# Seven products of quarters in place of eight for the q, k and v of each attention head

## What is computed

```
h = _rmsnorm(x, norm1_g[l])                      # 512 x 2048
proj = h @ w_in[l]
q, k, v, og, gkf, gkb, glu, ga, gb = jnp.split(proj, offsets, axis=-1)
qh = _to_heads(q, GLA_HEADS) * (GLA_DK ** -0.5)  # 4 heads of 256 columns
kh = _to_heads(k, GLA_HEADS)                     # 4 heads of 256
vh = _to_heads(v, GLA_HEADS)                     # 4 heads of 512
log_af = jax.nn.log_sigmoid(gkf @ gla_gk_fwd_w[l] + gla_gk_fwd_b[l]) / GLA_GATE_NORMALIZER
...
o_f = _gla_scan(qh, kh, vh, _to_heads(log_af, GLA_HEADS), False)
```

## Time and profile before

| | us |
|---|---|
| median of 3 runs | 4249.54 |
| lowest, highest | 4245.31, 4250.67 |
| the profiled execution's own time | 4248.95 |
| its span, first to last instruction | 4247.2 |
| TensorE busy in the span | 3640.4 (86%) |
| VectorE busy | 2771.0 (65%) |
| ScalarE busy | 921.1 (22%) |
| GpSimd busy | 1251.8 (29%) |
| TensorE in one of the four heads, q to the last output, head 0 | 29.73 to 164.26 |

### The profile page before, as it was taken

How to read it: one execution, slowest core, us unless ns; L and a number is a source line. 1 busy time by engine, 2 the same in 40 slices (tenths; PEclk the granted TensorE clock), 3 DMA queues, 4 the chain that set the end, 5 groups by cost and what they waited for, 6 DMA issues and landing times.

```text
span 4247.2 us, 39184 instructions
## 1 busy us (share of the span) xinstructions
PE 3640.4 (86%) x13406; PEld 2204.9 (52%) x13406; DVE 2771.0 (65%) x4163; ACT 921.1 (22%) x2049; POOL 1251.8 (29%) x768
## 2 busy tenths in 40 slices
PE   9999999999999989868699999789998777555555
PEld 3444479545766667645588886444443334211111
DVE  3233359102999999974866667875656878766666
ACT  2232210101222211132211121111111233233222
POOL 0000000000233332231223323233323555666665
PEclk9999999999999999889899999899999899899999
DMA  3111248888999999999999999999999999999998
GB/s 136 60 56 64 70 169 299 300 315 292 390 416 397 389 419 409 412 373 411 407 409 412 415 426 418 423 421 427 427 404 385 418 414 402 402 419 418 418 418 361
DMA packets 162496, 1488.41 MB, mean 350 GB/s; under 512 B 24512, under 2 KB 24640, under 8 KB 33344
## 3 DMA queue, kind: packets, MB, share of 16 engines
q0 software_dynamic: 81408, 948.08, 53.8%
q1 hardware_dynamic: 70704, 512.44, 31.0%
q10 hardware_dynamic: 10256, 26.35, 1.6%
HBM read 1465.82 MB, written 20.97 MB: 350 GB/s over the span
## 4 chain that ended last, share of the span: by engine, by line
PE 58%; DMA 27%; DVE 9%; issue 5%; ACT 1%; POOL 0%; SPq 0%; ACTq 0%; DVEq 0%; POOLq 0%
PE bank L1750 34%; DMA arena_c<-in_peer_uv_rest,arena_c 14%; PE bank L2081 6%; PE bank L1801 5%; PE bank L1854 5%; DVE arena_o L1436 4%; DMA wring<-in_peer_u_tiles 4%; DMA wring<-in_w_in 3%; DMA arena_c<-in_peer_uv,arena_c 3%; PE bank L1898 2%; PE bank L1816 1%; PE bank L1940 1%; DVE arena_c L1423 1%; DMA wring<-in_conv_w_pw 1%; DMA wring<-in_w_out 1%
## 5 line engine op out<-in xcount | busy, mean ns | idle before, releaser
L1750 PE MATMUL bank<-arena_h,wring 128*128 128x128 f32 (+5 forms) x6784 | 1408.4, 371 | 48.7 <-DMA wring<-in_w_in 19.1
L687 POOL DMA_INDIRECT arena_c<-in_peer_uv,arena_c x272 | 662.1, 2434 | 2599.4 <-DVE arena_o L1436 1526.1
L1750 PEld LDWEIGHTS bank<-arena_h,wring 128*128 128x128 f32 x6784 | 1049.1, 195 | 405.3 <-issue 135.5
L1423 DVE SCALAR_TENSOR_TENSOR arena_c<-arena_c 128x2048 f32<-128x2048 f32 (+1 forms) x512 | 915.1, 1787 | 291.0 <-DMA arena_c<-in_peer_uv_rest,arena_c 252.4
L1436 DVE SCALAR_TENSOR_TENSOR arena_o<-arena_c,arena_o 128x2048 f32<-128x2048 f32 (+1 forms) x511 | 944.5, 1848 | 222.0 <-ACT arena_c L862 163.9
L2111 PE MATMUL bank<-arena_c,cols 128*128 128x512 f32 x960 | 518.3, 668 | 358.2 <-ACT cols L1046 358.1
L2111 PEld LDWEIGHTS bank<-arena_c,cols 128*128 128x128 f32 x960 | 178.5, 204 | 673.9 <-ACT cols L1046 540.2
L2081 PE MATMUL bank<-wring,arena_h 128*128 128x512 f32 x1024 | 445.5, 594 | 17.0 <-DMA wring<-in_peer_u_tiles 17.0
L698 POOL DMA_INDIRECT cols<-dots,cols x240 | 339.2, 1414 | 116.0 <-issue 100.1
L856 ACT ACTIVATE arena_c<-arena_c 128x1 f32<-128x1 f32 x272 | 55.1, 203 | 1380.2 <-DVE arena_c L1423 1365.2
L2081 PEld LDWEIGHTS bank<-wring,arena_h 128*128 128x128 f32 x1024 | 192.6, 190 | 268.3 <-issue 234.3
(11 more groups left out here) (227 smaller groups left out, 2367.9 us busy)
## 6 DMA issues: line engine op xcount, KB each, us to landing
wring<-in_w_in SPq DMA_DIRECT2D x176, 1024.0 KB, 10.8
wring<-in_peer_u_tiles SPq DMA_DIRECT2D x64, 1024.0 KB, 17.6
wring<-in_w_out SPq DMA_DIRECT2D x48, 1024.0 KB, 9.9
wring<-in_peer_w_q SPq DMA_DIRECT2D x48, 1024.0 KB, 11.1
wring<-in_gla_w_o SPq DMA_DIRECT2D x32, 1024.0 KB, 11.3
wring<-in_conv_w_pw SPq DMA_DIRECT2D x32, 1024.0 KB, 12.7
wring<-in_w_v SPq DMA_DIRECT2D x16, 1024.0 KB, 4.9
wring<-in_w_ga SPq DMA_DIRECT2D x16, 1024.0 KB, 4.9
```

The costliest lines, as they stand in the source:

```text
L687: pool.indirect_dma_start(out=slot_of(n), out_offset=None, in_=uv_tab, in_offset=column(idx_cur, U % 2, k)).then_inc(landed(n)[0], 16)
L1423: V.scalar_tensor_tensor(row, row, 1.0, block_of(h2, n // P)[:, first:], ALU.mult, ALU.mult, accum_out=act_u[:, n % TOP:n % TOP + 1]).then ...
L1750: last = M(ps[bank][:, at:at + hi - lo], w_tile(slot)[:, k, :], act_in[:, k, lo:hi], start=k == 0, stop=k == KT - 1)
```

## The change

A product of two matrices, each cut in two by two quarters, takes eight products of quarters. The change computes it with seven, by Strassen's scheme in Winograd's form, for q, k and v of every head: the names P1 to P7 are the seven products, S1, S2, S4 sums of quarters of weights, h_1 to h_4 sums of quarters of `hT`, and U2, C11, C12, U3, C22, C21 the sums that make results.

- VectorE makes h_1 to h_4 once, behind the normalisation (2048 columns each).
- GpSimd makes four sums of 1024 columns for q, four for k, and four for each of two chunks of v, in every head. The fourth is written over a quarter of the tile itself.
- TensorE's seven products of q and of k are 8 matmuls of 256 columns each, those of v 16. They come in the order P1, P2, P5, P6, P3, P7, P4 and take the banks 4 to 7 in turn.
- ScalarE copies P1 and P5 out, and VectorE adds the others (`add_out`), 7 operations for each of q, k and v: of 256 columns for q and k, of 512 for v.
- The first load of the ring is four tiles in place of three, and the loads of v come in another order.

The core of the diff:

```diff
+            def weight_sums(n, set_of, a11, a12, a21, a22):
+                s1, s2, s4 = set_of
+                G.tensor_tensor(s1, a21, a22, ALU.add).then_inc(w_sum, 1)
+                pool.wait_ge(w_sum, n + 1)
+                G.tensor_tensor(s2, s1, a11, ALU.subtract).then_inc(w_sum, 1)
+                pool.wait_ge(w_sum, n + 2)
+                G.tensor_tensor(s4, a12, s2, ALU.subtract).then_inc(w_sum, 1)
+                G.tensor_tensor(a21, a11, a21, ALU.subtract).then_inc(w_sum, 1)
...
+                for chunk in range(2):
+                    slot = 2 * chunk
+                    pool.wait_ge(w_in_slot[slot], 16 * (turn + 1))
+                    pool.wait_ge(w_in_slot[slot + 1], 16 * (turn + 1))
+                    pool.wait_ge(mm, product_count(h, chunk, P3))
+                    weight_sums(h * SUMS + 8 + 4 * chunk, [by_cols(a) for a in sum_sets[chunk]],
...
-                for n in range(4):
-                    act.wait_ge(q_mm, h * 4 + (n + 1))
-                    dst = qT[:, n, :] if n < 2 else kT[:, n - 2, :]
-                    A(dst, ps[4 + n][:], ACT.Copy, scale=DK ** -0.5 if n < 2 else 1.0).then_inc(q_ev, 1)
+                for which in range(2):
+                    copy_out(which, P1, 0, 0)
+                    copy_out(which, P5, 1, 1)
...
                     act.wait_ge(z_qk, h * 4 + (u + 1))
-
-                for b in range(NB):
-                    act.wait_ge(v_mm, h * 4 + (b + 1))
-                    A(v_tok[:, b, :], ps[4 + b][:], ACT.Copy).then_inc(v_ev, 1)
+                    if u == 2:
+                        copy_out(2, P1, 0, 0)
+                copy_out(2, P5, 1, 1)
...
+            dve.wait_ge(n1_done, KT)
+            V.tensor_tensor(h_1, lower[:, :, token_half(1)], lower[:, :, token_half(0)], ALU.subtract).then_inc(n1_done, 1)
...
+                def add_out(which):
+                    dve.wait_ge(copied, h * COPIES + (2 * which + E1))
+                    add_product(which, U2, P6, (0, 0), (1, 0))
+                    add_product(which, C11, P2, (0, 0), (0, 0))
+                    dve.wait_ge(copied, h * COPIES + (2 * which + E5))
+                    add_quarter(which, C12_PART, (1, 0), (0, 1), (1, 1))
+                    add_product(which, C12, P3, (0, 1), (0, 1))
+                    add_product(which, U3, P7, (1, 0), (1, 0))
+                    add_quarter(which, C22, (1, 0), (1, 1), (1, 1))
+                    add_product(which, C21, P4, (1, 0), (1, 0))
...
+                def v_wait(n):
+                    if n < 4:
+                        added_by(1, (U2, C12, U3, C21)[n])
+                    if n == P3:
+                        copied_by(2, E1)
+                    if n == P7:
+                        added_by(2, C11)
+                    if n == P4:
+                        copied_by(2, E5)
...
+                first = seven(0, q_wait, (weight_half(0, 0), weight_half(0, 1), weight_half(1, 0), weight_half(1, 1)),
+                              sum_sets[0], lambda *to: half_product(*to, normed=h == 0))
+                if h:
+                    first[P1].then_inc(w_used, 1)
+                first[P4].then_inc(w_used, 1)
+                first = seven(1, k_wait, (weight_half(2, 0), weight_half(2, 1), weight_half(3, 0), weight_half(3, 1)),
+                              sum_sets[1], half_product)
+                first[P4].then_inc(w_used, 2)
```

More of the change, by code:

```diff
@@ L59 @@
 HEAD_TILES = 8
+HALF_TILE = TILE // 2
+(P1, P2, P5, P6, P3, P7, P4) = range(7)
+(E1, E5) = (1, 2)
+(U2, C11, C12_PART, C12, U3, C22, C21) = range(1, 8)
+PRODUCTS, COPIES, ADDS = 21, 6, 21
+SUMS = 16
 SB_GLU0 = HEADS * HEAD_TILES
@@ L270, in hybrid_block @@
         glow = take(T)
-        assert o_[0] <= SG, o_[0]
+        h_1, h_2, h_3, h_4 = (take(KT // 2, T // 2) for _ in range(4))
+        q_s4, k_s1 = take(HALF_TILE), take(HALF_TILE)
+        assert o_[0] <= SG + 1932, o_[0]
+        q_s1, q_s2 = (view(arena_o, (KT - 4) * T + n * HALF_TILE, HALF_TILE) for n in range(2))
+        pair_flat = pair_w.rearrange("p j t -> p (j t)")
+        k_s2, k_s4 = (pair_flat[:, n * HALF_TILE:(n + 1) * HALF_TILE] for n in range(2))
+        sum_sets = ((q_s1, q_s2, q_s4), (k_s1, k_s2, k_s4))
+        sq_flat = sq_o.rearrange("p e t -> p (e t)")
+        rstd_x = sq_flat[:, 0:T]
+        wgk = sq_flat[:, T:T + KT * (32 + RANK)].rearrange("p (k r) -> p k r", r=32 + RANK)
         sig0 = view(arena_c, RU, 2, 2, GL)
@@ L1732, in gate_ranks @@
                 for k in range(4 * c, 4 * c + 4):
-                    last = M(ps[6][0:32 + RANK, :], wgk[:, k, :], hT[:, k, :], start=k == 0, stop=k == KT - 1)
+                    last = M(ps[1][0:32 + RANK, :], wgk[:, k, :], hT[:, k, :], start=k == 0, stop=k == KT - 1)
                 last.then_inc(glow_mm, 1)
@@ L1773, in heads_sum @@
                 pe.wait_ge(o_added, h + 1)
[L1774 to L1785 removed]
+                M(ps[6][:], ones_d, sq_o[:, 0, :], start=True, stop=True).then_inc(o_stat, 1)
@@ new lines, in _, with seven @@
+            halves = hT[:, 0:KT // 2, :], hT[:, KT // 2:KT, :]
+            def seven(which, waits, weights, sums, product):
+                first = []
+                for n, (w, tokens) in enumerate((
+                        (weights[0], halves[0][:, :, token_half(0)]), (weights[1], halves[1][:, :, token_half(0)]),
+                        (sums[0], h_1), (sums[1], h_2), (sums[2], halves[1][:, :, token_half(1)]),
+                        (weights[2], h_3), (weights[3], h_4))):
+                    waits(n)
+                    first.append(product(w, tokens, bank_of(which, n), n))
+                return first
@@ L1793, in _ @@
                       start=True, stop=True).then_inc(z_mm, 1)
-                pe.wait_ge(q_ev, h * 4 + 4)
-                for s in range(4):
-                    tile_ready(4 + s, h, HEAD_TILES)
-                    for k in range(QUART):
-                        kk = s * QUART + k
-                        for b in range(NB):
-                            last = M(ps[4 + b][:], hT[:, kk, b * P:b * P + P], w_quart(s)[:, k, :],
-                                     start=kk == 0, stop=kk == KT - 1)
-                            if k == 0 and b == 0:
-                                last.then_inc(w_used, 1)
-                            if kk == KT - 1:
-                                last.then_inc(v_mm, 1)
+                first = seven(2, v_wait, [[weight_cols(n, j), weight_cols(n + 2, j)] for n, j in
+                                          ((0, 0), (1, 0), (0, 1), (1, 1))],
+                              [[sum_sets[n][i].rearrange("p (k c) -> p k c", c=DV // 2) for n in range(2)]
+                               for i in range(3)], v_product)
+                first[P1].then_inc(w_used, 1)
+                first[P4].then_inc(w_used, 3)
                 pe.wait_ge(z_qk, h * 4 + 4)
```

138 lines of the change are left out of this document (119 added, 19 removed).

## The result

The changed kernel takes 4310.55 us (median of 4 runs, 4307.18 to 4315.61), the kernel before, on the same chip, 4248.03. The ratio is 1.0139 with a 95% interval of [1.0125, 1.0153]: slower by 62.5 us. The profiled execution took 4315.61 us, its span 4313.9.

What follows compares the result with a forecast made beforehand. PE was taken to bound the kernel, with the decay chain 12.7 us of slack behind it. Head 0 at +28.9 us and heads 1 to 3 at +33.9 gave +62.8 on 4248.95, about 4312; range 4256 to 4330.

Steps and rivals of the forecast that it cites:

- The matmuls saved: PE in each head: seven products for eight gain 6.3 us in q and k and 6.3 in v, 50 in all.
- Z: Start of a head's decay matmuls on PE, 84.86 us in head 0 before the change; times in v count from it.
- v without any contention: v of each head: waits on the decay chain alone start the scores 5.2 us later, so a head wins only 1.1 us.
- GpSimd's sums: GpSimd, sixteen sums a head: each sum of 1024 columns was put at 2.3 us.
- Whom they hold: First decay turn beside v's sums: each sum holds VectorE's operations with two SBUF inputs to its end, 12.4 us in all.
- D: Delay of VectorE's first decay turn by GpSimd's sums in v: 12.4 us.
- P3, P7, scores: v of each head: P3 starts at Z+45.6, P7 at Z+58.9, scores at Z+74.6, against Z+57.0: +17.6 us a head.
- The long wait: PE's wait before P3 in v: 15.6 us, with 3.0 us more for the slower clock behind it.
- The start of head 0: Normalisations held by GpSimd's sums end 11.8 us late, at 50.1; q ends at 71.7 instead of 57.3: +14.4 us.
- Sum: All four heads: head 0 +28.9 us, heads 1 to 3 +33.9, together +62.8.
- The rival of a kernel with no hold: GpSimd's sums don't delay VectorE, only waits on the decay chain remain: 4249 us, give or take 5; chance 0.13.
- The rival of a faster kernel: ScalarE's copy and C11 stand ready when PE comes in v, so product time alone counts: 4203 us; chance 0.03.

Runs made afterwards that it cites:

- e1: Changed kernel with every GpSimd sum shortened to four columns (q, k and v left wrong): 4253.13 us, ratio 1.0001.
- e2: Changed kernel with only the sums of v shortened to four columns, those of q and k whole (v left wrong): 4261.34 us, ratio 1.0021.
- e8: Changed kernel with every GpSimd sum cut into four instructions of 256 columns, nothing left out: 4285.52 us, ratio 1.0072.
- e3: Changed kernel with GpSimd's sums replaced by memsets of the same 1024 columns (q, k and v wrong): 4254.62 us, ratio 1.0005.
- e7: Changed kernel with e4's order and e1's four-column sums together (q, k and v wrong): 4214.52 us, ratio 0.9905.
- e9: Changed kernel with first decay matmul and turn's start ahead of k, v's copies, U2 and C11 earlier, k's head 0 sums later: 4226.47 us, ratio 0.9932.
- e4: Changed kernel, in v ScalarE's copy of P1 behind the first decay turn, P5, U2 and C11 behind the second, nothing left out: 4255.19 us, ratio 1.0.

## Why the prediction was right

The forecast of 4312 us stands against 4310.55, and the mechanism was the one forecast. By its steps (head 0, then the others):

- **The matmuls saved.** Right. q and k of head 1 take 49.3 us from 190.08 to Z at 239.38, where they took 55.9: -6.6 for a forecast of -6.3, and nothing of a weight sum or an add shows there.
- **v without any contention.** Right, and shown apart by e1 and e2: P3 at Z+33.4 (forecast 33.2), P7 at Z+46.3 (46.5), scores at Z+63.2 (62.2). The last is 1.0 late: P7 and P4 took 17.1 us behind the 5.7 us wait where I put 15.7.
- **GpSimd's sums.** 2.35 us undisturbed, for an estimate of 2.3. That the number came so close is luck in part. I scaled the 0.29 us of an instruction of 128 columns by eight, and with it whatever part of it doesn't grow with the columns. The runs show such a part in a sum: 4 columns take 0.20 us (e1), 256 take 0.70 (e8), 1024 take 2.35, so about 0.2 us and 2.1 ns a column. How the affine select splits was not measured.
- **Whom they hold.** Shown. The delay of P3 against e1 is 45.3-33.4 = 11.9 for D = 12.4, and the operations of VectorE's first turn in the result, less the same ones before, add up to the same 11.9. But the parts of D are not the forecast ones, and that its total held is luck in part. GpSimd began at Z+2.2, not Z+1.4, so one sum and a half were done when L1248 began, not two. The operation of three columns (L1263) was not held. Up to the clamp the delay was 9.2 us, where the forecast put 11.7; the products behind it (L1271, L1274) took 2.7, where it put 0.7. Nor does it take semaphores between VectorE's operations, by which I had let a sum in after each: the normalisations don't wait for each other, and about five of them are done in the 15.1 us to the end of the last sum, beside five sums and the rest of a sixth, but eleven in the 7.2 us behind it. One row had spoken against a hold, VectorE's operations on time beside a DMA issue; e3 shows that not every GpSimd instruction holds: memsets, which read nothing, leave the adds and the scan alone. Why the DMA issue doesn't was not tested. The difference between sums and memsets is what the Trainium skill states in "SBUF — State Buffer", section "Who interferes with whom": two SBUF inputs on VectorE contend with a GpSimd instruction that reads SBUF, not with one that only writes; by that rule VectorE's operations with two inputs lose nothing in e3, and the trace agrees (an add of 0.69 us beside a memset).
- **P3, P7, scores.** Z+45.3, 58.1 and 73.7, for 45.6, 58.9 and 74.6; in heads 1 to 3 the scores are at Z+75.0. The long wait cost 2.0 us of clock in P3 of head 0 (9.06 for 7.07) and 2.6 to 2.7 in heads 1 to 3 (9.69 to 9.79), not 3.0. The short one cost more than the 1.7 forecast there: P7 and P4 take 17.0 us in heads 1 to 3, 3.0 over their 14.0, and 15.77 in head 0. These misses are of opposite sign and mostly cancel.
- **The start of head 0.** Norms end at 49.8 (forecast 50.1), h_1 at 52.1; q ends at 69.6 for 71.7, since PE's wait for h_1 was 1.7 us and cost no clock.
- **Sum.** Head 0: +25.8 in the place of 28.9. Heads 1 to 3: +34.3 in the place of 33.9. Together 60.1 of 62.8.

One small term stood nowhere: PE waits 0.7 to 2.0 us in each head for the second tile of v, 4.2 us in all. I had tiles landing in time for it. In the changed kernel it costs nothing, since the wait before P3 is shorter by as much (11.4 us in head 2, where the tile took longest, 14.4 in the others, with P3 at Z+45.2 or 45.3 in all); in e7 and e9 it costs time.

The rival of a kernel with no hold was 4249, give or take 5, no change. e1 and e3 are that kernel: 0.5 and 2.0 us over the kernel before. The rival of a faster kernel needed the third turn's end before Z+29.3 or a copy that doesn't stand behind it; e4 gave the second, and e7 the silent GpSimd as well: 4214.52, 39 of the 46 us.

What stays open: the heads account for 60.1 us, the spans of the same two executions differ by 66.7, and the medians by 62.5; what lies behind the heads, 2.4 or 6.6 us, was not looked for. That ScalarE's operations are never held was seen in these traces and not tested.

## What to carry to other kernels

A saving on the engine that bounds a kernel is worth only what the chain behind it has in slack: measure that chain to its end (here 12.7 us) before you count the saving, and look at what stands in the queue ahead of each new release. Work that is put on an idle GpSimd, and that reads as these sums do, is free only while VectorE does nothing with two operands in SBUF and no clamp like this one; one sum of 2.35 us turned a four-column operation into one of 2.31. Where two causes each hide the other's cure, undo them one at a time and then together, since e1 and e4 each gave nothing over the kernel before and together (e7) 39 us. With the whole computation the most that was reached is 26 us (e9).

## What the hardware showed that I had not expected

- A hold is spread over durations, not over gaps: VectorE's operation begins on time in the trace and is long. Busy time of VectorE rose for it from 2771.0 to 2883.4 us, new adds included, and says nothing of work done.
- GpSimd's memsets held one kind of VectorE operation after all, the clamp, which works on 512 columns in 0.43 us where an add takes 0.69: 0.98 beside memsets. The Trainium skill, "SBUF — State Buffer", section "Who interferes with whom", has a TensorScalar in a two-port mode contend with any GpSimd instruction; that this clamp runs in such a mode is read from its speed, no run here shows it.
- A whole sum between two VectorE operations lengthened the second by 1.97 to 2.15 us, less than its own 2.35; a quarter of a sum by 0.34 to 0.52, less than its 0.70. So a part of each GpSimd instruction's span seems not to hold; which part was not looked for.
